# Second query chunk of both cross attentions as products over 64 rows, the two halves of the array by turns into two banks that VectorE adds

## The reference

```python
def memory_cross_attention(h, mem_n, wq, wk, wv, wo):
    q = (h @ wq).reshape(b, s, X_HEADS, X_HEAD_DIM)
    k = (mem_n @ wk).reshape(b, -1, X_HEADS, X_HEAD_DIM)
    v = (mem_n @ wv).reshape(b, -1, X_HEADS, X_HEAD_DIM)
    logits = jnp.einsum('bshd,bmhd->bhsm', q, k).astype(jnp.float32) * X_HEAD_DIM ** -0.5
    p = jax.nn.softmax(logits, -1).astype(v.dtype)
    return jnp.einsum('bhsm,bmhd->bshd', p, v).reshape(b, s, X_HEADS * X_HEAD_DIM) @ wo

for l in range(DEPTH):                       # DEPTH is 2
    x = x + 0.5 * rmsnorm(swiglu(rmsnorm(x, g[0]), ...), g[1])
    x = x + rmsnorm(mixer_l(rmsnorm(x, g[2])), g[3])
    x = x + rmsnorm(memory_cross_attention(rmsnorm(x, g[4]), ...), g[5])
    x = x + 0.5 * rmsnorm(swiglu(rmsnorm(x, g[6]), ...), g[7])
```

## Time and profile before

| what | value |
|---|---|
| median of 3 runs | 1085.67 us |
| the profiled execution's own time | 1085.41 us |
| its span | 1083.7 us |
| TensorE matmuls busy | 1070.7 us (99%), 6172 instructions |
| TensorE weight loads busy | 938.9 us (87%), 6172 instructions |
| VectorE busy | 776.0 us (72%) |
| ScalarE busy | 564.6 us (52%) |
| granted TensorE clock | 0.999 of full speed |

### The profile page before, as it was taken

The page is one execution under the profiler, slowest core; times in us unless marked ns, Lnnn a source line. Parts: engine busy times, 40 slices in busy tenths (PEclk is TensorE's granted clock), DMA queues, the critical chain, the costliest instruction groups (busy, mean ns, idle before and its releaser), DMA issues.

```text
span 1083.7 us, 16043 instructions
## 1 busy us (share of the span) xinstructions
PE 1070.7 (99%) x6172; PEld 938.9 (87%) x6172; DVE 776.0 (72%) x1015; ACT 564.6 (52%) x816; POOL 67.8 (6%) x169
## 2 busy tenths in 40 slices
PE   8999999999999999999999999999999999999997
PEld 7888888998889888888888888888978989888886
DVE  5966769875886786676778667678487768676675
ACT  6534446667766753443465344345466666443442
POOL 3000010110020200000010000002100101000000
PEclk9999999999999999999999999999999999999999
DMA  8756474564144365644536564453804435745641
GB/s 322 249 192 222 165 273 132 170 205 151 50 184 152 108 247 199 228 166 183 194 108 246 209 233 159 190 194 108 272 14 143 175 117 195 252 159 191 222 165 40
DMA packets 50155, 194.59 MB, mean 180 GB/s; under 512 B 4496, under 2 KB 24480, under 8 KB 31792
## 3 DMA queue, kind: packets, MB, share of 16 engines
q1 hardware_dynamic: 48832, 189.54, 49.2%
q0 software_dynamic: 1264, 4.25, 1.4%
HBM read 192.73 MB, written 1.05 MB: 179 GB/s over the span
## 4 chain that ended last, share of the span: by engine, by line
PE 91%; DVE 5%; ACT 2%; issue 1%; DMA 1%; POOL 0%; SPq 0%; POOLq 0%; ACTq 0%; DVEq 0%
PE psum L960 21%; PE psum L1076 21%; PE psum L968 11%; PE psum L941 5%; PE psum L1061 3%; PE psum L1298 3%; PE psum L946 3%; PE psum L784 2%; PE psum L786 2%; PE psum L785 2%; PE psum L980 1%; PE psum L1267 1%; PE psum L1168 1%; PE psum L810 1%; PE psum L811 1%; PE psum L809 1%
## 5 line engine op out<-in xcount | busy, mean ns | idle before, releaser
L2322 DVE TENSOR_TENSOR w_ring<-raw,w_ring 128x2048 fp32r<-128x2048 f32 (+2 forms) x120 | 272.8, 2273 | 25.4 <-ACT w_ring L1656 25.1
L1656 ACT ACTIVATE w_ring<-raw 128x2048 fp32r<-128x2048 f32 x121 | 230.7, 1907 | 47.3 <-DMA raw<-in_ffn_w_gate 25.3
L2439 DVE TENSOR_REDUCE work<-psum 128x256 f32<-128x512 f32 x172 | 114.4, 687 | 175.3 <-PE psum L968 161.2
L960 PE MATMUL psum<-h_both,w_ring 128*128 128x512 f32 x1024 | 237.3, 389 | 0.0
L960 PEld LDWEIGHTS psum<-h_both,w_ring 128*128 128x128 f32 x1024 | 192.2, 188 | 39.9
L1076 PE MATMUL psum<-w_ring,g_both 128*128 128x512 f32 x936 | 220.0, 390 | 0.0
L1076 PEld LDWEIGHTS psum<-w_ring,g_both 128*128 128x128 f32 x936 | 173.2, 188 | 34.3
L1754 ACT ACTIVATE V<-work 128x512 f32<-128x512 f32 x44 | 27.9, 634 | 249.3 <-DVE work L2448 249.3
L968 PEld LDWEIGHTS psum<-h_both,w_ring 128*128 128x128 f32 x1024 | 127.1, 192 | 2.5
L968 PE MATMUL psum<-h_both,w_ring 128*128 128x256 f32 x1024 | 127.9, 283 | 0.0
L2322 DVE TENSOR_TENSOR w_ring<-QT,w_ring 128x2048 fp32r<-128x2048 f32 x40 | 91.4, 2285 | 2.4 <-ACT w_ring L1656 2.4
(11 more groups left out here) (336 smaller groups left out, 1560.7 us busy)
## 6 DMA issues: line engine op xcount, KB each, us to landing
raw<-in_ffn_w_gate SPq DMA_DIRECT2D x43, 1024.0 KB, 4.8
raw<-in_ffn_w_up SPq DMA_DIRECT2D x43, 1024.0 KB, 4.8
QT<-in_ffn_w_down SPq DMA_DIRECT2D x40, 1024.0 KB, 4.8
raw<-in_ab_w_in SPq DMA_DIRECT2D x7, 1024.0 KB, 5.5
gain_row<-in_norm_g POOLq DMA_DIRECT2D x8, 512.0 KB, 6.6
raw<-in_ffn_w_down SPq DMA_DIRECT2D x4, 1024.0 KB, 4.7
raw<-in_xa_wk SPq DMA_DIRECT2D x4, 1024.0 KB, 4.8
raw<-in_ab_w_out SPq DMA_DIRECT2D x4, 1024.0 KB, 5.0
```

The costliest lines, as they stand in the source:

```text
L960: nc.tensor.matmul(outs[-1][:, :], hi[:, k, P * j:P * (j + 1)], h_both[:, k].rearrange("p a n -> p (a n)"), start=(k == 0), stop=False)
L1656: nc.scalar.activation(w_hi[:, c % RING, 0:k * n], raw_at(c)[:, 0:k * n], ACT.Copy)\
L2322: nc.vector.tensor_tensor(w_lo[:, c % RING, 0:k * n], raw_at(c)[:, 0:k * n], w_hi[:, c % RING, 0:k * n].bitcast(F32), ALU.subtract).then_i ...
L2439: nc.vector.tensor_reduce(dst[:, p % 2, TOK * j:TOK * (j + 1)], bank(name).rearrange("p (a n) -> p n a", a=2), AX.X, ALU.add)\
```

## The change

`xq{l}.1` of both cross attentions is no longer made by `feature_major` but by a new function `row_halves`. Each of its 48 matmuls becomes two: one over rows 0 to 63 (partitions 0 to 63 of weights and tokens) into the ticket `xq{l}.1`, and one over rows 64 to 127 into a new ticket `xq{l}.1b`, one after the other by turns. ScalarE copies `xq{l}.1` to `QT` as before; a new VectorE instruction then adds the bank of `xq{l}.1b` to those columns of `QT`. The scores of `u1` wait for that addition instead of for ScalarE's copy. All later tickets move on by one bank in the first cross attention, and by one more in the second.

```diff
--- before.py
+++ after.py
@@ -168,7 +168,7 @@
         u = units_of(f"xa{l}")
         fill(s)
         xv = XA_FILL[l]
-        out.extend([f"xq{l}.0", f"xq{l}.1", f"score{u[0]}", f"score{u[1]}"] +
+        out.extend([f"xq{l}.0", f"xq{l}.1", f"xq{l}.1b", f"score{u[0]}", f"score{u[1]}"] +
                    [f"score{u[2]}", xv[0], f"pT{u[0]}"] +
                    xv[1:] + [f"pT{u[1]}", f"score{u[3]}", f"pv{u[0]}", f"pv{u[1]}",
                     f"pT{u[2]}", f"pT{u[3]}", f"pv{u[2]}", f"pv{u[3]}"])
@@ -842,6 +842,22 @@
                     last = feature_terms(out_[:, TOK * j:TOK * (j + 1)], hi, lo, a_hi, a_lo, j)
                 filled(name, last)
 
+            def row_halves(name):
+
+                hi, lo = weights(C[name])
+                outs = [take(name), take(name + "b")]
+                for j in range(2):
+                    cols = slice(P * j, P * (j + 1))
+                    for k in range(KT):
+                        for w, a in ((hi, h_hi), (hi, h_lo), (lo, h_hi)):
+                            for r, out_ in enumerate(outs):
+                                rows = slice(64 * r, 64 * (r + 1))
+                                last = nc.tensor.matmul(out_[:, TOK * j:TOK * (j + 1)], w[rows, k, cols], a[rows, k, :],
+                                                        start=(k == 0 and w is hi and a is h_hi),
+                                                        stop=(k == KT - 1 and w is lo))
+                                if j and k == KT - 1 and w is lo:
+                                    filled(name + "b" * r, last)
+
             def first_gate(name, s):
 
                 c = C[name]
@@ -1302,10 +1318,10 @@
                 u0, u1, u2, u3 = units_of(f"xa{l}")
                 begin(s)
                 first_features(f"xq{l}.0", s)
-                feature_major(f"xq{l}.1", h_hi, h_lo)
+                row_halves(f"xq{l}.1")
                 ready(f"xq{l}.0")
                 scores(u0)
-                ready(f"xq{l}.1")
+                ready(f"xq{l}.1b")
                 scores(u1)
                 xv = XA_FILL[l]
                 scores(u2)
@@ -2586,6 +2602,10 @@
             def cross(l, s):
                 u0, u1, u2, u3 = units_of(f"xa{l}")
                 split_to(C[XA_FILL[l][0]])
+                dve.wait_ge(*full(f"xq{l}.1b"))
+                dve.wait_ge(*freed[f"xq{l}.1"])
+                q = QT[:, 2:4, :].rearrange("p h n -> p (h n)")
+                nc.vector.tensor_tensor(q, q, bank(f"xq{l}.1b"), ALU.add).then_inc(freed[f"xq{l}.1b"][0], 1)
                 split_to(C[XA_FILL[l][0]] + 1)
                 row_max(u0)
                 row_max(u1)
```

## The result

The changed kernel took 1091.5 us (median of 4 runs, 1090.79 to 1092.1) against 1085.63 us (4 runs, 1085.3 to 1085.98): 1.0052 times as long, 95% interval 1.004 to 1.0064. Measured again on another occasion (experiment 1) it took 1.0038 times as long, 1.0025 to 1.0051. It is slower.

What follows compares the result with a forecast made beforehand. TensorE was taken to bound the kernel (1070.7 us busy, 91% of the chain). Products 0, going in 2 x 0.2, waits 2.35 + 1.55: +4.3 on 1085.4 gives 1089.7 us; own range 1088.1 to 1091, wide range 1087.9 to 1101.5.

Steps and rivals of the forecast that it cites:

- the rival with turns: Loads or products of the two halves take turns at both sites: +14.5 to +15.8 us, 1099.9 or 1101.2; chance 0.3.
- The products: The 96 half products at each site: pairs run side by side at 120 ns, difference 0, bounds -0.6 to +5.8 us.
- the four column tiles: Gates' products over 32 columns: a round of four costs one whole-array matmul, 216 ns; carried over to row halves.
- The load of 128 columns for 64 rows: Weight loads of the halves, 113 ns each, might queue for one another: +5.1 us a site.
- Into and out of the tiling: Entering the half-row mode costs 0.2 us a site (0 to 0.3); leaving is hidden by the next wait.
- The first cross attention: The addition delays the low part of `xv0.1` on VectorE, so TensorE's value products come late: +2.35 us.
- The covers that I had named: First site: late transposes covered with 2.4 us left, output rows after `xo0.1` with 1.4; transfers by spare time.
- The second: Second cross attention: value products 0.7 us late, then transposes wait for late probabilities; +1.55 us in all.
- The sum: Whole change: 0 for the products, 2 x 0.2 for going in, 2.35 + 1.55 for waits: +4.3 us.
- Faster by a cost that goes with the rows: A pair takes less than 120 ns because operand reading bounds; at 60 ns the time is 1083.9; chance 0.04.
- Given back later: No-difference rival: TensorE's 3.9 us of waits half taken back further on, products gain 1.25; 1086.5, chance 0.06.

Runs made afterwards that it cites:

- experiment 1: The changed kernel again with no edit, against the kernel before; median 1090.57 us, 1.0038 times as long.
- experiment 5: Changed kernel with all 48 products of rows 0 to 63 first, then all 48 of rows 64 to 127; 1.0125 times the kernel before.
- Experiment 4: Changed kernel's 96 half products without the addition, a tiny VectorE read behind the low part freeing the second bank; 1.0007 times the kernel before.
- Experiment 2: Changed kernel with the addition moved behind the low part in VectorE's queue; 1.0017 times the kernel before.
- experiment 3: Changed kernel with 48 whole products over 128 rows into two banks instead of halves, same addition at the same place; 1.0038 times the kernel before.
- experiment 6: Changed kernel with three products of one half, then three of the other, instead of strict turns; 1.0049 times the kernel before.

## Why the prediction was right

The prediction of 1089.7 us, slower, held, but not to the letter. The first measurement, 1091.5, is 1.8 above it and 0.5 above the forecast's own range of 1088.1 to 1091; it lies only in the wide range, which reached to 1101.5 for the sake of the rival with turns. Of the 1.8 us 1.2 do not lie at the sites. The second measurement, 1090.57, is within the forecast's own range. The cost of the sites, which leaves the start of the program out, is 4.68 us against 4.3.

**The products.** Right. Pairs side by side, 5.73 us against 5.64 before; the difference forecast was 0. Carrying over the four column tiles to halves of the rows was the step with the most at stake, since by turns it was forecast to be over 10 us dearer; experiment 5 costs 9.4 us more. The load of 128 columns for 64 rows did not bind: in the trace the loads of a pair start 3 ns apart, so loads of the two halves overlap as those of the column tiles did. Of the two sentences of the Trainium skill that were weighed, that of TensorEngine Tiling (Key Properties), that tiles load and multiply in parallel, agrees with 96 products in 5.73 us. What the Trainium skill (TensorE: Matmul & The Clock Gate, LDWEIGHTS) says, that a load's time goes by its columns and not its rows, agrees with the length of a load here, 188 ns for 64 rows and 192 for 128, and it changed nothing.

```profile
L855 PEld LDWEIGHTS psum<-h_both,w_ring x192: 182/188/188, 330.9 to 869.2; 64*128 64x128 f32 x192
```

**Into and out of the tiling.** 0.2 a site was forecast. The first scores start 336.85 - 329.86 = 6.99 us after the last matmuls of `xq0.0` begin, before 334.58 - 327.86 = 6.72: 0.27 a site, of which the part for leaving is covered by the wait behind it, as was said. Experiment 4, which has no such wait, shows 0.34 and 0.27.

**The first cross attention.** Right in mechanism and size. From the second scores on: addition, low part of `xv0.1`, the load for the value products at 341.62 instead of 337.04, 4.58, less the 2.00 of the start 2.58 us late; forecast 2.35 + 0.2. The load side stands idle for 1.64 us there, forecast 1.6. Experiment 2 shows what the queue place costs, 1.09 of the 2.47 us, and experiment 3 that nearly all of the cost is there without halves. The covers that I had named, the transposes, the low part of `xo0.1` and the transfers, all held: at the products with the values the shift was still 2.47.

**The second.** Right in mechanism, with one wait missed. The second scores and the transposes came as forecast but a little cheaper, about 1.5 us together instead of 1.75. The transposes started at 876.32 - 4.48 = 871.84, where the forecast had 871.8; it had counted from the load at 870.25 and not from the matmul 0.1 later, and put the 0.2 for going in on top of a wait that takes most of it up. Then 0.6 more at the scores of `u3`, for the bank of `u2`. In the kernel before its release came at 873.2 and the scores at 874.1, in the timeline:

```profile
873.20 0.16 DVE L2567 RECIPROCAL einv<-esum 128x2 f32<-128x2 f32 x1
...
874.10 0.38 PE L1267 MATMUL psum<-XK,QT 128*128 128x256 f32 x1
```

The softmax 2.8 us later against a TensorE 1.5 later used that up. I had followed the shift of the softmax to `prob_transposes` and the output rows, and not to the bank. That it goes with the late softmax is shown by experiment 2, where the softmax of `u2` is 0.8 us late, no later than TensorE, and the second site costs 0.95 with nothing after its second scores.

**The sum** of 4.3 us came within 0.4 of 4.68. That is closer than its terms, since they missed both ways: the second site lacked the wait for the bank, 0.6 us, and the terms for going in and for the transposes were 0.3 too large together.

**The rivals.** Turns of the halves: refuted for the changed kernel by its own 5.73 us. Faster by a cost that goes with the rows: refuted by experiment 5. Given back later: between the two sites the shift moved by 0.01 us.

## What to carry to other kernels

Products over 64 rows in two halves of the array cost together what one product over 128 rows costs; where the full 128 rows are there to be summed they give nothing, and the second bank with its addition is pure cost. An instruction that waits for the last result of a stage belongs behind all that its engine can do without that result; here the same addition one chunk further down VectorE's queue took the change's cost from 4.7 to 2.3 us. When a stage is made late, follow it not only to its readers but also to the buffers that it releases.

## What was not expected of the hardware

TensorE does not keep matmuls of different halves of the rows in the order of the program. Three of one half in a row, then three of the other, ran as fast as strict turns (5.74 against 5.73 us for 96). The starts in runs of six, twelve and 48 (6.07, 8.80, 11.10 us) fit a reach of four: one product of a half running and three waiting while the other half's go ahead, or products up to four places behind the oldest unfinished one, which give the same times here. A half that has stood idle takes 0.22 us from its first product to its second, and 0.12 from then on. How the engine does that no run shows. The Trainium skill (TensorE: Matmul & The Clock Gate, The mechanism) says that matmuls start and end strictly in order and that only weight loads are pulled ahead; the 5.74 us of experiment 6 do not agree with it.
